# Expert rows added up in DRAM by the DMAs themselves, and a last stage that adds onto rows of bias

## What is computed

```python
s = sigmoid(xt @ router_w); sel = s + router_b
# two experts per token, out of the best group of four
gate = take(s, eidx); gate = gate / gate.sum(-1, keepdims=True)
for e in range(16):
    hid = silu(xt @ w_gate[e]) * (xt @ w_up[e])
    out = out + combine[:, e:e + 1] * (hid @ w_down[e])
x = layer_norm(ALPHA * x1 + out, ln2_w, ln2_b)      # ALPHA = 2 ** 0.25
```

## Time and profile before

| | |
|---|---|
| median of 3 runs | 1034.89 us |
| lowest and highest | 1032.19, 1034.9 us |
| span of the profiled execution, first to last instruction | 1030.7 us |
| own time of the profiled execution | one like the three runs, 1.5 to 4.2 us more than the span |
| busy: TensorE, VectorE, ScalarE, GpSimd | 884.6, 667.7, 455.7, 139.0 us |
| mean granted TensorE clock | 0.931 of full |
| moved by DMA | 202.25 MB |

### The profile page before, as it was taken

One profiled execution on the slowest core, in us unless ns is written; L12 is line 12 of the kernel. 1 busy time (PEld: TensorE's weight loads), 2 busy tenths in 40 slices (PEclk: granted clock), 3 DMA queues, 4 the chain that ended last, 5 costly groups with the idle time before them and its releaser, 6 DMA issues.

```text
span 1030.7 us, 15075 instructions
## 1 busy us (share of the span) xinstructions
PE 884.6 (86%) x4992; PEld 772.3 (75%) x4992; DVE 667.7 (65%) x981; ACT 455.7 (44%) x594; POOL 139.0 (13%) x168
## 2 busy tenths in 40 slices
PE   6999999999967999995199999999999999998000
PEld 6998887888755888884189898988989898897000
DVE  3441899983265778874837586676898662635695
ACT  3531110102355443313336686767888662645231
POOL 3000011011112112100100001000110100000583
PEclk9999999999996999996599999999999999999555
DMA  7620213314225433314657498695999863595671
GB/s 270 214 83 1 99 54 123 105 73 160 82 85 164 157 108 100 125 41 160 229 224 284 167 405 345 219 392 181 413 407 410 339 224 142 185 324 205 212 259 79
DMA packets 77509, 202.25 MB, mean 196 GB/s; under 512 B 7215, under 2 KB 27009, under 8 KB 77473
## 3 DMA queue, kind: packets, MB, share of 16 engines
q1 hardware_dynamic: 63984, 155.31, 41.8%
q0 software_dynamic: 9888, 33.76, 9.1%
q10 hardware_dynamic: 3600, 12.72, 3.1%
HBM read 167.14 MB, written 34.62 MB: 196 GB/s over the span
## 4 chain that ended last, share of the span: by engine, by line
PE 79%; DVE 9%; issue 7%; DMA 2%; ACT 1%; POOL 1%; DVEq 0%; SPq 0%; POOLq 0%; ACTq 0%
PE banks L1072 17%; PE banks L622 13%; PE banks L611 13%; PE banks L636 13%; PE banks L1069 8%; PE banks L1186 6%; PE banks L595 2%; DVE arena L849 2%; PE banks L1207 2%; PE banks L602 1%; PE banks L1053 1%; DMA arena<-in_x 1%; DVE split_weights L804 1%; PE banks L1121 1%; DVE small L865 1%
## 5 line engine op out<-in xcount | busy, mean ns | idle before, releaser
L804 DVE TENSOR_TENSOR split_weights<-arena,split_weights 128x1024 fp32r<-128x1024 f32 x192 | 223.7, 1218 | 1.0
L654 ACT ACTIVATE split_weights<-arena 128x1024 fp32r<-128x1024 f32 x192 | 190.7, 1052 | 12.2 <-ACT work L691 10.4
L1072 PE MATMUL banks<-split_weights 128*128 128x512 f32 (+2 forms) x960 | 182.5, 351 | 0.0
L1072 PEld LDWEIGHTS banks<-split_weights 128*128 128x128 f32 x960 | 156.2, 191 | 23.9 <-issue 1.4
L622 PE MATMUL banks<-split_weights,split_rows 128*128 128x256 f32 x1152 | 147.5, 284 | 0.0
L622 PEld LDWEIGHTS banks<-split_weights,split_rows 128*128 128x128 f32 x1152 | 142.7, 191 | 1.9
L611 PE MATMUL banks<-split_weights,split_rows 128*128 128x512 f32 x576 | 136.0, 392 | 2.5 <-DVE split_rows L808 2.5
L636 PE MATMUL banks<-split_weights,split_hidden 128*128 128x512 f32 x576 | 137.5, 394 | 0.0
L611 PEld LDWEIGHTS banks<-split_weights,split_rows 128*128 128x128 f32 x576 | 109.1, 190 | 25.6 <-issue 2.9
L636 PEld LDWEIGHTS banks<-split_weights,split_hidden 128*128 128x128 f32 x576 | 106.6, 188 | 21.6
L821 DVE TENSOR_TENSOR work<-work,banks 128x256 f32<-128x256 f32 x48 | 20.2, 421 | 116.0 <-PE banks L622 116.0
(11 more groups left out here) (294 smaller groups left out, 991.2 us busy)
## 6 DMA issues: line engine op xcount, KB each, us to landing
arena<-in_w_gate SPq DMA_DIRECT2D x64, 512.0 KB, 6.2
arena<-in_w_up SPq DMA_DIRECT2D x64, 512.0 KB, 7.2
arena<-in_w_down SPq DMA_DIRECT2D x64, 512.0 KB, 7.9
y_scratch<-work ACTq DMA_DIRECT2D x24, 512.0 KB, 6.6
arena<-in_w_in SPq DMA_DIRECT2D x20, 512.0 KB, 5.5
arena<-in_x SPq DMA_DIRECT2D x16, 512.0 KB, 6.1
arena<-in_w_out SPq DMA_DIRECT2D x8, 512.0 KB, 5.1
x_scratch<-arena SPq DMA_DIRECT2D x8, 512.0 KB, 3.4
```

What stands on the lines that cost most here:

```text
L654: act.activation(unit_split(u, 0), unit_slot(u), AF.Copy).then_inc(xw_hi, 1)
L804: dve.tensor_tensor(unit_split(u, 1), unit_slot(u), unit_split(u, 0).bitcast(F32), ALU.subtract).then_inc(xw_lo, 1)
L1072: last = pe.matmul(b[:, 0:width], xT[:, hx, k, j * P:(j + 1) * P], wc[:, hw, k, 0:width], start=(k == 0 and i == 0), stop=(k == KC - 1 and ...
```

## The change

Rows of the experts are summed in DRAM. There is a second copy of x1, `acc_dram`, with 128 spare rows ahead for unused slots. ScalarE multiplies a tile's result by each slot's gate (already divided by ALPHA) while it copies it out of PSUM, and GpSimd issues an indirect DMA that adds the rows of the tile onto the rows of their tokens. Since LayerNorm doesn't mind a factor, x1 + out / ALPHA is normalised, with the epsilon divided by ALPHA squared. In the last stage SP loads the sums, VectorE takes statistics and does one pass (subtract the mean, multiply by the weight), ScalarE multiplies by the reciprocal of the deviation, and GpSimd issues DMAs that add the result onto output rows into which SP has written the bias before. The gates by slot need a further one-hot product, in three bfloat16 parts, and unused slots are pointed at the spare rows, one row each.

```diff
@@ SP, mixer
+            sp.wait_ge(made, 3)
+            for rows_out in (x1_dram, acc_dram):
+                sp.dma_start(rows_out[0:P, :]..., ones...).then_inc(rows_filled, 16)
...
             def store_x1(ch):
                 sp.wait_ge(x1_ready, ch.c + 1)
-                sp.dma_start(x1_dram[bass.ds(ch.c * P, P), :], x1s).then_inc(x1_out, 16)
+                for rows_out in (x1_dram, acc_dram):
+                    sp.dma_start(rows_out[bass.ds(P + ch.c * P, P), :], x1s).then_inc(x1_out, 16)
@@ SP, experts
-            with sp.Fori(tiles, TILES_MAX + 1) as i:          # fills of the unused rows of y_dram
...
+            sp.wait_ge(y_out, ADDED)
+            for t in range(T):
+                sp.dma_start(out_tiles[t], ln2[:, 1, :]).then_inc(bias_out, 16)
             sp.wait_ge(xw_lo, UNITS * NE)
-            for t in range(SETS):
-                reload_x1(t)
+            sp.wait_ge(acc_done, 1)
             for t in range(T):
...
+                sp.dma_start(final(t), acc_dram[P + t * P:P + (t + 1) * P, :]).then_inc(acc_in[t], 16)
@@ GpSimd
+            def add_rows(g):
+                pool.wait_ge(y_out, ADDED + 16 * g)
+                pool.tensor_copy(tok_out, tok_sums[:, bass.ds(g, 1)]).then_inc(out_idx_ready, 1)
+                pool.wait_ge(y_sb, PRIMED + g + 1)
+                wait_apart(pool, out_idx_ready, g + 1)
+                pool.indirect_dma_start(out=acc_dram, out_offset=bass.IndirectOffsetOnAxis(ap=tok_out, axis=0), in_=ys,
+                                        in_offset=None, compute_op=ALU.add).then_inc(y_out, 16)
+
+            def body(e, g, last, more):
+                gather(g + 1)
+                add_rows(g)
...
-            total = each_tile(pool, "pool", lambda e, g, last, more: gather(g + 1))
+            for i, src in enumerate((ln2_w[0], ln2_b[0])):
+                pool.dma_start(ln2[:, i, :], src.partition_broadcast(P)).then_inc(y_out, 16)
+            pool.wait_ge(sum_index_ready, 1)
+            total = each_tile(pool, "pool", body)
...
+            wait_apart(pool, y_out, ADDED + total * 16)
+            pool.sem_inc(acc_done, 1)
+            pool.wait_ge(bias_out, 16 * T)
             for t in range(T):
-                if t + 3 < T:
-                    fetch(t + 3)
-                pool.wait_ge(scaled_ready, t + 1)
-                pool.tensor_tensor(final(t, 0), final(t, 0), ln2[:, 1, :], ALU.add).then_inc(out_ready, 1)
+                pool.wait_ge(out_ready, t + 1)
+                pool.dma_start(out_tiles[t], final(t), accum_op=ALU.add).then_inc(stored, 16)
+            pool.wait_ge(stored, 16 * T)
@@ TensorE
+            pe.wait_ge(gate_hot_ready, 1)
+            for i in range(2 * T):
+                last = pe.matmul(bank(3)[:, 0:96], hot_lo[:, i, :], hot_gate[:, i, :], ...)
+            last.then_inc(gate_sums_ps, 1)
             transpose_rows(0)
@@ ScalarE
-                act.wait_ge(y_out, PRIMED + g * 16)
-                act.activation(ys, psum[:, 2:4, :]..., AF.Copy).then_inc(y_sb, 1)
-                act.wait_ge(y_sb, PRIMED + g + 1)
-                act.dma_start(y_dram[bass.ds(g * P, P), :], ys).then_inc(y_out, 16)
+                act.wait_ge(y_out, ADDED + g * 16)
+                act.activation(ys, psum[:, 2:4, :]..., AF.Copy, scale=gate_slot[:, bass.ds(g, 1)]).then_inc(y_sb, 1)
...
+            act.wait_ge(gates_ready, 1)
             each_tile(act, "act", body, own)
...
             for t in range(T):
                 act.wait_ge(fin_stats, t + 1)
-                act.activation(rs_f[:, t:t + 1], mv_f[:, t, 1:2], AF.Sqrt, bias=LN_EPS).then_inc(fin_std, 1)
-                if t + 2 < T:
-                    scale_x1(t + 2)
+                act.activation(rs_f[:, t:t + 1], mv_f[:, t, 1:2], AF.Sqrt, bias=LN_EPS / ALPHA ** 2).then_inc(fin_std, 1)
+                act.wait_ge(fin_mid, t + 1)
                 act.wait_ge(fin_rstd, t + 1)
-                act.activation(final(t, 1), final(t, 2), AF.Identity, scale=rs_f..., bias=shift_f...).then_inc(fin_norm, 1)
+                act.activation(final(t), final(t), AF.Copy, scale=rs_f[:, t:t + 1]).then_inc(out_ready, 1)
@@ VectorE, routing
+            dve.wait_ge(tok_ready, 1)
+            own.link(dve.tensor_scalar(unused, tok[:, :], 0.0, i_tok, ALU.is_equal, ALU.mult))
+            dve.tensor_tensor(tok_sums[:, :], tok[:, :], unused, ALU.add).then_inc(sum_index_ready, 1)
...
+            own.link(dve.tensor_copy(gate_parts[:, 0], gflat2))
+            own.link(dve.tensor_tensor(gate_rest, gflat2, gate_parts[:, 0], ALU.subtract))
+            own.link(dve.tensor_copy(gate_parts[:, 1], gate_rest))
+            own.link(dve.tensor_tensor(gate_parts[:, 2], gate_rest, gate_parts[:, 1], ALU.subtract))
+            for i in range(3):
+                last = dve.tensor_tensor(hot_gate[:, :, i * 32:(i + 1) * 32], hot_tile, gate_parts[:, i]..., ALU.mult)
+            last.then_inc(gate_hot_ready, 1)
...
-            for u in range(6):
+            for u in range(2):
+                split_lo(0, u)
+            dve.wait_ge(gate_sums_ps, 1)
+            own.link(dve.tensor_copy(gate_sum, bank(3)[:, 0:96]))
+            own.link(dve.tensor_tensor(gate_sum[:, 32:64], gate_sum[:, 32:64], gate_sum[:, 64:96], ALU.add))
+            dve.tensor_tensor(gate_slot, gate_sum[:, 0:32], gate_sum[:, 32:64], ALU.add).then_inc(gates_ready, 1)
+            for u in range(2, 6):
                 split_lo(0, u)
@@ VectorE, last stage: instead of two gated adds, statistics, L859, L860 and L872
+            for t in range(T):
+                dve.wait_ge(acc_in[t], 16)
+                for i in range(2):
+                    last = dve.bn_stats(st_c[:, i, :], final(t)[:, i * 512:(i + 1) * 512])
+                wait_apart(dve, dve_own, own.done(last))
+                dve.bn_aggr(mv_f[:, t, :], st_c).then_inc(fin_stats, 1)
+                dve.wait_ge(fin_stats, t + 1)
+                dve.scalar_tensor_tensor(final(t), final(t), mv_f[:, t, 0:1], ln2[:, 0, :], ALU.subtract, ALU.mult).then_inc(fin_mid, 1)
+                r = rs_f[:, t:t + 1]
+                dve.wait_ge(fin_std, t + 1)
+                dve.reciprocal(r, r).then_inc(fin_rstd, 1)
```

More of the change, by code:

```diff
@@ L68 @@
 PRIMED = 1
+ADDED = 32
 class Chunk:
@@ L321, in hybrid_kernel @@
         packed_sum = at("c", 2)[0:1]
+        gate_rest = at("c", 2 * T)
+        gate_sum = at("c", 96)
+        unused = at("c", 32)
+        gate_parts = at("c", 24).bitcast(BF16).rearrange("p (i n) -> p i n", i=3)
+        hot_gate = at("c", 48 * T * 2).bitcast(BF16).rearrange("p (i n) -> p i n", n=96)
+        used["d"] = 3072
         sil = at("d", DE)
@@ L640, in body @@
                 last.then_inc(y_ps, 1)
+            pe.wait_ge(gate_hot_ready, 1)
+            for i in range(2 * T):
+                last = pe.matmul(bank(3)[:, 0:96], hot_lo[:, i, :], hot_gate[:, i, :], start=(i == 0), stop=(i == 2 * T - 1))
+            last.then_inc(gate_sums_ps, 1)
             transpose_rows(0)
@@ L783, in dve_experts @@
             for i in range(2):
-                last = dve.tensor_tensor(hot_hi[:, i * T:(i + 1) * T, 32:64], hot_tile[:, i * T:(i + 1) * T, :], over(i_lo[:, 0:T], 32), ALU.mult)
+                last = dve.tensor_tensor(hot_hi[:, i * T:(i + 1) * T, 32:64], hot_tile[:, i * T:(i + 1) * T, :], over(i_lo[:, 1:T + 1], 32), ALU.mult)
             last.then_inc(hot_ready, 1)
@@ L844, in dve_experts @@
             each_tile(dve, "dve", body, own)
-            def gated(t, i):
-                xr = final(t, 2)
-                return dve.scalar_tensor_tensor(xr, final(t, i), gatew[:, i, t:t + 1], xr, ALU.mult, ALU.add)
-            for t in range(T + 1):
-                if t < T:
-                    dve.wait_ge(x1_scaled, t + 1)
-                    dve.wait_ge(y_in[t % SETS], 32 * (t // SETS + 1))
-                    first = own.done(gated(t, 0))
-                if t > 0:
-                    r = rs_f[:, t - 1:t]
-                    dve.wait_ge(fin_std, t)
-                    own.link(dve.reciprocal(r, r))
-                    dve.scalar_tensor_tensor(shift_f[:, t - 1:t], mv_f[:, t - 1, 0:1], -1.0, r, ALU.mult, ALU.mult).then_inc(fin_rstd, 1)
-                if t < T:
-                    dve.wait_ge(dve_own, first)
-                    own.link(gated(t, 1))
-                    for i in range(2):
-                        last = dve.bn_stats(st_c[:, i, :], final(t, 2)[:, i * 512:(i + 1) * 512])
-                    wait_apart(dve, dve_own, own.done(last))
-                    dve.bn_aggr(mv_f[:, t, :], st_c).then_inc(fin_stats, 1)
-                if t == 1:
-                    dve.wait_ge(ln2_in, 32)
-                if t > 0:
-                    dve.wait_ge(fin_norm, t)
-                    dve.tensor_tensor(final(t - 1, 0), final(t - 1, 1), ln2[:, 0, :], ALU.mult).then_inc(scaled_ready, 1)
+            dve.wait_ge(y_out, ADDED)
+            for t in range(T):
[9 more added lines that the diff above has]
+                dve.reciprocal(r, r).then_inc(fin_rstd, 1)
         @block.sync
```

(2 more changed lines are left out.)

87 lines of the change are left out of this document (30 added, 57 removed).

## The result

The changed kernel takes 1127.3 us (median of 4 runs, 1119.85 to 1129.75) and the kernel before 1033.54 us on the same chip (4 runs, 1031.11 to 1034.9): a ratio of 1.09, interval 1.0859 to 1.094. It is 9% slower, where I had forecast 13 us less. The profiled execution spans 1123.6 us, 92.9 more than before.

What follows compares the result with a forecast made beforehand. TensorE was taken to bound the kernel, other engines counting only where it waits. Routing +4, tiles +17 and last stretch -34 gave -13 us, from 1034.9 to a median of 1022; range 1004 to 1040 at 8 in 10.

Steps and rivals of the forecast that it cites:

- What bounds the kernel: Whole kernel: TensorE sets the end for 79% of the span; work taken from other engines counts only where TensorE waits.
- Routing, +4.0: Ahead of TensorE's first expert tile: new small VectorE operations and three products add 4.0 us, bounds 3 and 5.
- Per tile, +17: Expert tiles: gathers behind scatters stall TensorE 1.2 us in each of 14 boundary tiles, +17 us, bounds 6 and 35.
- 0.97 of issue: Expert tiles, GpSimd: issuing the adding scatter takes 0.97 us, starting at S + 2.35 (S: tile's start on TensorE).
- The landing: Boundary tiles: gather issued at S + 5.0, its rows seen at S + 12.65, against S + 11.42 wanted by TensorE.
- Rival 2: Boundary tiles: TensorE waits behind the adding scatter, 14 us per microsecond of stall, kernel slower; chance 0.20.
- threshold of 2.1 us of stall: Boundary tiles: stall per tile from which the tiles' loss decides against the last stage's gain, (34 - 4)/14.
- Last stretch, -34: From the last eviction's start to the program's end: 47.8 us against 81.7, so -34 us, bounds -37 and -21.
- The tail: End of the program: it ends 5.3 us after the last output store lands.
- Rival 3: Last stage: adding output DMAs at 4.8 us each set its pace, median 1035 us; chance 0.10.
- rival 1: Expert tiles: gathers come early enough, tiles cost +0 to +5 us, time 1007 us; chance 0.20.
- rival 4: Last stage: loads or statistics replace GpSimd, VectorE at 5.3 us a tile, little gain, 1039 us; chance 0.05.

Runs made afterwards that it cites:

- Kernel 1: The changed kernel with GpSimd issuing each tile's gather ahead of the scatter of the tile before; 1006.3 us, ratio 0.9749 to the kernel before.
- kernel 5: The changed kernel with VectorE waiting for its own split before starting the next one; 1091.7 us in one run.
- kernel 8: Kernel 1 with the output stored plainly by SP, without adding or bias; 996.32 us, ratio 0.9664 to the kernel before.
- kernel 9: Kernel 1 with the output stored plainly by GpSimd, without adding or bias; 1002.28 us, ratio 0.9715 to the kernel before.
- kernel 11: Kernel 1 with SP instead of GpSimd waiting for the last output DMAs; 1002.82 us, ratio 0.9713 to the kernel before.

## Why the prediction was wrong

**What bounds the kernel.** Right: only what keeps TensorE waiting counts. Kernel 1 carries slower scatters than the sum assumed, and loses nothing in the tiles.

**Routing, +4.0.** Measured +3.5. The new operations stand where they were put, and the three products take 1.89 us together (2.0).

**Per tile, +17: the step that failed.** The chain of the prediction was right in its places: the eviction, the scatter, the loop's step, the gather, TensorE's need at S + 11.4. Two of its numbers were not.

1. *"0.97 of issue".* I took the scatter's issue from the row of a gather. An adding scatter takes 1.6, and up to 6.9 where it meets a VectorE run without a gap, as it can in boundary tiles: VectorE was busy for 16.57 of 18.04 us there. This is the family of the long waits, seven of 7.6 to 9.0 us, 58.1 in all.
2. *The landing.* The gather was to land at S + 12.65, 7.65 us behind its issue. In the tile of 848.26 it was issued at S + 5.7 and its rows were read at S + 15.4: 9.7 us. This is the family of the short waits: seven of 3.5 to 4.9 us, 27.2 in all, where I had 1.2 each. (The eighth, 4.25 us at 1064.05, has a long issue and no loads beside it.) GpSimd's queue in this tile shows which terms were short (packets, MB, share; 855.6 to 859.9, which is the scatter, then 859.9 to 863.0, the gather, by their packets):

```profile
q0 software_dynamic: 136, 0.53, 62.2%
...
q0 software_dynamic: 148, 0.50, 40.9%
```

The scatter's data begin at S + 7.3 (I had 6.05) and take 4.3 us (3.5); the gather's take 3.1 (2.4), and its rows are read 0.6 later (0.7). The gather did keep its 41% of the engines. Too small were the start of the queue's work (by 1.3 us), the scatter (by 0.8) and the gather itself beside the loads (by 0.7). In the tile of 1048.22, with no weights to load, the scatter's data took some 3.4 us, so the 3.5 was right for a scatter alone.

And a term was missing: behind 14 of the 15 waits TensorE's clock was at half for 3 to 6 us, 31.7 us in all. Rival 2 had the right place and the right sign (TensorE waiting behind an adding scatter), and even its price, 14 us per microsecond of stall, turns out low: a mean wait of 6.0 us in 15 tiles cost 121, or 20 a microsecond. Its threshold of 2.1 us of stall was passed almost threefold. What I held against it, that the gathers' queue gets its share whatever the weights want, is true of the queue and says nothing of the order within it.

**Last stretch, -34.** Measured -32.0. Its parts: 11.2 to the first statistics (11.5), 3.2 a tile (2.93), adding output landed at 42.5 (about 41.6 moved). The tail was wrongly read: I took 5.3 us as a distance from the last store's landing, and kernels 8 and 9 show it as about 8 us from GpSimd's last work. Since the change gives GpSimd the last work, it showed in full: 49.7 for 47.8. Rival 3 was half right. The adding outputs do fill the DMA engines, but they keep up with VectorE's tiles of 2.93 us: the last one stops moving some 5 us after its issue began. Rivals 1 and 4 fell: no boundary tile had its rows in time, and nothing but VectorE set the pace behind the first load.

## What to carry to other kernels

When a new DMA is put on a queue that also feeds the critical engine, the order on that queue is the first thing to cost: issue the transfer that somebody waits for ahead of the one that waits for somebody, and here 9% slower becomes 2.5% faster. Don't price a GpSimd DMA by the row of another kind of DMA, or by one beside a VectorE with gaps, nor a stall by its length alone where it also takes TensorE's clock. At the end of a program, GpSimd's last work should be early.

## What the runs showed of the hardware

- An indirect DMA that reads SBUF took GpSimd 1.6 us to issue (0.99 without the add) and up to 6.9 inside a run of VectorE instructions without a gap (in the changed kernel and kernel 1, 16 of 24 such issues took 6.3 to 6.9 and eight 2.3; with gaps of 0.2 us in kernel 5, none over 2.5). The gather of 853.97, which reads DRAM, took 1.13 beside a gapless run of four.
- An adding DMA moves about half the bytes in the engines' time: 209 GB/s at a share of 1.07 (kernel 1's outputs), against 407 at 1.02 (the kernel before, a boundary tile).
- After 3.79 us without work TensorE came back at half its clock, and had the full one again 5 us later. After 3.77 us it came back at full and fell to half 1.3 us later; after 3.54 us it did not fall.
- The span ended 8.0 us after GpSimd's last instruction in the kernel before, 8.1, 8.5 and 8.3 after the last data of the DMAs that it waited for in the changed kernel and kernels 1 and 9, and 9.3 after its last issue in kernel 11.
